# Rounded statistics of q and k and a new order of work in the opening of a hybrid decoder layer

## What is computed

```python
h = rmsnorm(x, g_mix)
q_sb, k_sb, v_sb, q_r, k_r, v_r, g_r, gate_sb, gate_ret = split_cols(h @ w_in)
q_sb = head_rmsnorm(to_heads(q_sb, SB_HEADS), sb_q_gain)      # 8 heads of 64
k_sb = head_rmsnorm(to_heads(k_sb, SB_HEADS), sb_k_gain)
y_sb = from_heads(stick_breaking_attention(q_sb, k_sb, to_heads(v_sb, SB_HEADS)))
q_r = rotary(to_heads(q_r, RET_HEADS)); k_r = rotary(to_heads(k_r, RET_HEADS)) * 0.125
y_r = retention_chunkwise(q_r, k_r, to_heads(v_r, RET_HEADS))
```

## Time and profile before

| | us |
|---|---|
| median of 3 runs (897.35 to 898.05) | 897.39 |
| the profiled execution's own time | 897.31 |
| its span, first to last instruction | 895.5 |
| TensorE busy | 887.5 (99%) |
| VectorE busy | 512.4 (57%) |
| ScalarE busy | 398.2 (44%) |
| GpSimd busy | 16.6 (2%) |

### The profile page before, as it was taken

One profiled execution on the slowest core, in us unless ns is written; L12 is line 12 of the kernel. 1 busy time (PEld: TensorE's weight loads), 2 busy tenths in 40 slices (PEclk: granted clock), 3 DMA queues, 4 the chain that ended last, 5 costly groups with the idle time before them and its releaser, 6 DMA issues.

```text
span 895.5 us, 11762 instructions
## 1 busy us (share of the span) xinstructions
PE 887.5 (99%) x4254; PEld 734.0 (82%) x4254; DVE 512.4 (57%) x644; ACT 398.2 (44%) x510; POOL 16.6 (2%) x19
## 2 busy tenths in 40 slices
PE   8999999999999999999999999999999999999998
PEld 6688888888888888888888888888888888888886
DVE  6797677677677443333556656566655643333444
ACT  6745756756755623232345333333333332323431
POOL 1500000000000000000000000000000000000000
PEclk9999999999999999999999999999999999999999
DMA  7224115115114252333223333322223333323141
GB/s 278 83 67 146 51 39 170 53 38 167 53 38 145 97 185 83 94 93 117 95 95 117 96 100 104 99 94 94 94 94 98 96 94 89 106 88 94 65 147 65
DMA packets 28699, 89.96 MB, mean 100 GB/s; under 512 B 3936, under 2 KB 5232, under 8 KB 28544
## 3 DMA queue, kind: packets, MB, share of 16 engines
q1 hardware_dynamic: 27376, 85.87, 30.1%
q10 hardware_dynamic: 1072, 3.67, 1.3%
q0 software_dynamic: 224, 0.06, 0.1%
HBM read 84.34 MB, written 2.10 MB: 97 GB/s over the span
## 4 chain that ended last, share of the span: by engine, by line
PE 96%; DVE 1%; DMA 1%; ACT 1%; issue 0%; SPq 0%; DVEq 0%
PE dense L424 30%; PE dense L426 29%; PE dense L425 29%; PE z L485 2%; PE aty L514 1%; DMA fs<-in_xT 1%; PE aty L425 1%; PE aty L426 1%; PE aty L424 1%; PE aty L529 1%; PE aty L531 1%; DVE fs L1228 0%; DVE w_lo L1228 0%; DVE lo L1231 0%; ACT hi L759 0%
## 5 line engine op out<-in xcount | busy, mean ns | idle before, releaser
L424 PE MATMUL dense<-hi,w_hi 128*128 128x512 f32 x1118 | 441.2, 395 | 1.4 <-DVE lo L1231 1.2
L425 PE MATMUL dense<-lo,w_hi 128*128 128x512 f32 x1118 | 435.4, 389 | 0.0
L426 PE MATMUL dense<-hi,w_lo 128*128 128x512 f32 x1118 | 435.3, 389 | 0.0
L1228 DVE TENSOR_TENSOR w_lo<-w_f,w_hi 128x1024 fp32r<-128x1024 f32 (+3 forms) x161 | 184.6, 1149 | 228.8 <-ACT w_hi L774 228.2
L424 PEld LDWEIGHTS dense<-hi,w_hi 128*128 128x128 f32 x1118 | 209.9, 188 | 50.7 <-issue 5.8
L426 PEld LDWEIGHTS dense<-hi,w_lo 128*128 128x128 f32 x1118 | 209.9, 188 | 44.4
L425 PEld LDWEIGHTS dense<-lo,w_hi 128*128 128x128 f32 x1118 | 210.1, 188 | 41.8 <-issue 0.7
L774 ACT CAST w_hi<-w_f 128x1024 fp32r<-128x1024 f32 (+2 forms) x159 | 157.5, 991 | 176.4 <-PE dense L426 174.3
L1228 DVE TENSOR_TENSOR fs<-fs 128x512 f32<-128x512 f32 (+3 forms) x115 | 86.8, 760 | 4.3 <-DMA fs<-fs 1.2
L759 ACT ACTIVATE fs<-fs 128x512 f32<-128x512 f32 (+2 forms) x75 | 54.5, 731 | 50.5 <-DVE fs L1231 38.6
L1228 DVE TENSOR_TENSOR lo<-fs,hi 128x512 fp32r<-128x512 f32 (+3 forms) x67 | 50.5, 762 | 37.2 <-ACT hi L1161 20.2
(11 more groups left out here) (118 smaller groups left out, 506.5 us busy)
## 6 DMA issues: line engine op xcount, KB each, us to landing
w_f<-in_w_in SPq DMA_DIRECT2D x52, 512.0 KB, 3.4
w_f<-in_w_up SPq DMA_DIRECT2D x44, 512.0 KB, 3.3
w_f<-in_w_down SPq DMA_DIRECT2D x16, 512.0 KB, 3.5
w_f<-in_w_b SPq DMA_DIRECT2D x8, 512.0 KB, 3.3
w_f<-in_w_out SPq DMA_DIRECT2D x8, 512.0 KB, 3.4
w_f<-in_w_pg SPq DMA_DIRECT2D x8, 512.0 KB, 3.3
w_f<-in_w_down SPq DMA_DIRECT2D x8, 384.0 KB, 3.1
fs<-in_xT SPq DMA_DIRECT2D x4, 512.0 KB, 7.3
```

Source lines behind the costliest of these rows:

```text
L424: mm(out, w1, x1, start=start, stop=False, skip_group_check=skip)
L425: mm(out, w1, x0, start=False, stop=False, skip_group_check=skip)
L426: return mm(out, w0, x1, start=False, stop=stop, skip_group_check=skip)
L1228: return nc.vector.tensor_tensor(out, a, b, op).then_inc(done, 1)
```

## The change

- The sums over the heads' squares of raw q and k are made in two rounded passes: ScalarE squares each twice, once rounded into `hi[:, T_FSQ + t]` and once in full, VectorE subtracts to `lo[:, T_FSQ + t]` (`first_square_low`), and TensorE multiplies both by the rounded block matrix `block_r`. That matrix is cast early, behind `raw_sum(3)`.
- TensorE makes the first of these sums behind block 1 of chunk 2 (before: behind block 6 of chunk 1), the second behind block 2 of chunk 2 (before: block 1). Five hooks of the first pair's `back` are one block later.
- On ScalarE `raw_square(0)` goes behind the rounding of chunk 1's weights, and `ahead(0, 2)` (chunk 4's weights) behind the split of q and k and the table load.
- On VectorE `constants()` and `ahead(0, 2)` go behind the norms, the split of q and k and the evacuation of v; only the scaled gain stays ahead.

```diff
--- before.py
+++ after.py
@@ -57,6 +57,7 @@
 T_AT = 27
 T_YQ = 27
 T_SQ = 31
+T_FSQ = 30
 T_X0 = 8
 T_M = 20
 T_G = 8
@@ -154,7 +155,7 @@
         s_rst, s_rln, s_rrs = sem("s_rst"), sem("s_rln"), sem("s_rrs")
         s_achi, s_aclo = sem("s_achi"), sem("s_aclo")
         s_w1hi, s_w1lo = sem("s_w1hi"), sem("s_w1lo")
-        s_fsq, s_xvar, s_fvar = sem("s_fsq"), sem("s_xvar"), sem("s_fvar")
+        s_fsq, s_fsqlo, s_xvar, s_fvar = sem("s_fsq"), sem("s_fsqlo"), sem("s_xvar"), sem("s_fvar")
 
         s_halo, s_c0, s_c1, s_c2, s_gelu = sem("s_halo"), sem("s_c0"), sem("s_c1"), sem("s_c2"), sem("s_gelu")
         s_g, s_ghi, s_glo = sem("s_g"), sem("s_ghi"), sem("s_glo")
@@ -453,9 +454,9 @@
 
             def first_stat(t):
 
-                pe.wait_ge(s_cst, 16)
-                pe.wait_ge(s_fsq, t + 1)
-                mm(z[:, t, :], cst[:, C_BLOCK, :], first_square(t), start=True, stop=True).then_inc(s_stat, 1)
+                pe.wait_ge(s_fsqlo, t + 1)
+                mm(z[:, t, :], block_r[:, :], hi[:, T_FSQ + t, :], start=True, stop=False)
+                mm(z[:, t, :], block_r[:, :], lo[:, T_FSQ + t, :], start=False, stop=True).then_inc(s_stat, 1)
 
             def stat_y(j):
 
@@ -614,10 +615,10 @@
                     return lambda: f(*a)
 
                 if prev is None:
-                    places = {(3, 0): at(sb_scores, j, 0), (3, 2): at(turn_v, 0, 2, (s_misc, 2)),
-                              (3, 7): at(sb_scores, j, 1), (4, 0): at(sb_turn, j, 0), (4, 5): at(sb_values, j, 0, 3),
+                    places = {(3, 1): at(sb_scores, j, 0), (3, 3): at(turn_v, 0, 2, (s_misc, 2)),
+                              (3, 7): at(sb_scores, j, 1), (4, 0): at(sb_turn, j, 0), (4, 6): at(sb_values, j, 0, 3),
                               (5, 1): at(sb_scores, j, 2), (5, 2): at(sb_turn, j, 1), (6, 0): at(sb_values, j, 0, 2),
-                              (6, 2): at(sb_turn, j, 2), (6, 5): at(sb_values, j, 0, 1), (6, 6): at(sb_values, j, 0, 0)}
+                              (6, 2): at(sb_turn, j, 2), (6, 6): at(sb_values, j, 0, 1), (6, 7): at(sb_values, j, 0, 0)}
                     first = 7
                 else:
                     places = {(3, 3): at(turn_v, j, 2, (s_misc, 3 * j + 1)), (3, 4): at(sb_scores, j, 0),
@@ -648,8 +649,8 @@
 
             warm_up()
             chunk(0, 0, 0, KD, T_X0, before={k: (s_xlo, k + 1) for k in range(KD)})
-            chunk(1, 1, 1, KD, T_X0, {6: lambda: first_stat(0)}, before={4: (s_wlo, 2)}, halved=True)
-            chunk(2, 2, 2, KD, T_X0, {0: stat_x, 1: lambda: first_stat(1)})
+            chunk(1, 1, 1, KD, T_X0, before={4: (s_wlo, 2)}, halved=True)
+            chunk(2, 2, 2, KD, T_X0, {0: stat_x, 1: lambda: first_stat(0), 2: lambda: first_stat(1)})
             back(0, None)
             with pe.Fori(1, PAIRS) as j:
                 front(j, j - 1, SLOTS * j)
@@ -782,6 +783,7 @@
 
             def first_square_of(t):
                 act.wait_ge(s_used, t + 1)
+                run(hi[:, T_FSQ + t, :], bank[t][:, :], ACT.Square, s_fsq)
                 run(first_square(t), bank[t][:, :], ACT.Square, s_fsq)
 
             act.wait_ge(s_gmix, 16)
@@ -791,11 +793,10 @@
                 if k % 2 == 0:
                     act.wait_ge(s_x[k // 2], 16)
                 run(hi[:, T_X0 + k, :], fs[:, A_X + k, :], ACT.Identity, s_xhi, scale=gain[:, G_MIX + k, :])
-                if k == 5:
-                    raw_square(0)
             act.wait_ge(s_wdma[1], 16)
             nc.scalar.copy(w_hi[1][:, 0:4, :], w_f[1][:, 0:4, :]).then_inc(s_w1hi, 1)
             nc.scalar.copy(w_hi[1][:, 4:8, :], w_f[1][:, 4:8, :]).then_inc(s_whi, 1)
+            raw_square(0)
             raw_square(1)
             raw_square(2)
             high(0, 2, first=True)
@@ -947,9 +948,9 @@
 
                 ahead(0, 1)
                 first_square_of(1)
-                ahead(0, 2)
                 act.wait_ge(s_xst, 1)
                 run(fs[:, A_G + 1, :], misc, ACT.Identity, s_xvar, scale=EPS * 64 / D)
+                act.wait_ge(s_fsqlo, 1)
                 run(fs[:, A_RS, :], misc, ACT.Ln, s_xln, scale=1.0 / D, bias=eps[:, :])
                 first_log(0)
                 act.wait_ge(s_xln, 1)
@@ -960,6 +961,7 @@
                 high_qk(0, 0)
                 high_qk(0, 1)
                 sigmoid_tables()
+                ahead(0, 2)
 
             def high_h(k):
                 act.wait_ge(s_hf, H_ORDER.index(k) + 1)
@@ -1270,21 +1272,33 @@
             low(0, 2)
             raw_sum(2)
             raw_sum(3)
+            dve.wait_ge(s_cst, 16)
+            nc.vector.tensor_copy(block_r[:, :], cst[:, C_BLOCK, :]).then_inc(s_cr, 1)
+
+            def first_square_low(t):
+
+                dve.wait_ge(s_fsq, 2 * t + 2)
+                if t == 0:
+                    dve.wait_ge(s_cr, 1)
+                tt(lo[:, T_FSQ + t, :], first_square(t), hi[:, T_FSQ + t, :], ALU.subtract, s_fsqlo)
+
+            first_square_low(0)
             low(1, 0)
-            def constants():
-
-                dve.wait_ge(s_cst, 16)
-                nc.vector.tensor_copy(ones_r[:, :], cst[:, C_ONES, :]).then_inc(s_cr, 1)
-                nc.vector.memset(mrev[:, 0:SEQ], 0.0).then_inc(s_cr, 1)
-                dve.wait_ge(s_cr, 2)
-                tt(mrev[:, 1:P + 1], cst[:, C_IDENT, ::-1], cst[:, C_IDENT, ::-1], ALU.mult, s_cr)
-                stt(cst[:, C_NEGU, :], cst[:, C_NEGU, :], 1.0, cst[:, C_IDENT, :], ALU.add, ALU.add, s_cr)
-                nc.vector.tensor_copy(block_r[:, :], cst[:, C_BLOCK, :]).then_inc(s_cr, 1)
-                dve.wait_ge(s_xacc, 3)
-                nc.vector.memset(fs[:, A_CP:A_CP + 2, 0:1], 0.0).then_inc(s_cr, 1)
+            first_square_low(1)
+            def scaled_gain():
+
                 dve.wait_ge(s_gain, 16 * 5)
                 g8 = gain[:, G_SBQ:G_SBQ + PAIRS, 0]
                 nc.vector.tensor_scalar(g8, g8, 0.125, None, ALU.mult).then_inc(s_cr, 1)
+
+            def constants():
+
+                nc.vector.tensor_copy(ones_r[:, :], cst[:, C_ONES, :]).then_inc(s_cr, 1)
+                nc.vector.memset(mrev[:, 0:SEQ], 0.0).then_inc(s_cr, 1)
+                dve.wait_ge(s_cr, 4)
+                tt(mrev[:, 1:P + 1], cst[:, C_IDENT, ::-1], cst[:, C_IDENT, ::-1], ALU.mult, s_cr)
+                stt(cst[:, C_NEGU, :], cst[:, C_NEGU, :], 1.0, cst[:, C_IDENT, :], ALU.add, ALU.add, s_cr)
+                nc.vector.memset(fs[:, A_CP:A_CP + 2, 0:1], 0.0).then_inc(s_cr, 1)
 
             def low_h(k):
                 dve.wait_ge(s_hhi, H_ORDER.index(k) + 1)
@@ -1469,15 +1483,17 @@
             def start():
                 first_variance(0)
                 first_variance(1)
-                constants()
-                dve.wait_ge(s_cr, 7)
-                ahead(0, 2)
+                scaled_gain()
+                dve.wait_ge(s_cr, 2)
                 first_norm(0)
                 first_norm(1)
                 low_qk(0, 0)
                 low_qk(0, 1)
                 dve.wait_ge(s_xrs, 1)
                 evac_x(2)
+                constants()
+                dve.wait_ge(s_cr, 7)
+                ahead(0, 2)
                 dve.wait_ge(s_rope, 16)
 
             def turned(j, t):
```

## The result

| | before | changed |
|---|---|---|
| median of 17 runs, us | 897.78 (897.29 to 898.35) | 900.19 (898.67 to 900.94) |
| ratio, 95% interval | | 1.0025 (1.0018 to 1.0033) |
| span of the profiled execution | 895.5 | 897.4 |
| mean granted clock of TensorE | 1.000 | 0.997 |

The changed kernel is 2.4 us slower, outside the range that was given (896.0 to 899.7). The mean clock of its executions is the first clue: two of the 17 have 1.000 and take 898.67 and 898.73 us, the other fifteen have 0.996 to 0.998 and take 899.20 to 900.94.

What follows compares the result with a forecast made beforehand. TensorE, busy 887.5 of 895.5 us, was the bound, with VectorE without slack from 34.40 to 59.8. VectorE's 1.0 us late minus 0.44 slack plus 0.2 restart gave +0.8: 897.31 to 898.1 us, range 896.0 to 899.7.

Steps and rivals of the forecast that it cites:

- the term for TensorE's clock: A lower TensorE clock behind the idle time at the second scores; left out of the forecast sum, priced at 1.8 us.
- rival 3: The 2.9 us stall at the second scores throws TensorE's clock to its lower level: 1.8 us more, 899.9 us, chance 0.08.
- The x part: Opening: moving ScalarE's first square of x behind the second chunk's rounding brings TensorE's start at 13.88 forward by 0.7 us.
- The new wait: TensorE reaches the sum of x squared at 20.8, VectorE's sum ends at 21.16: 0.4 us of new stall.
- Turns: Behind the norms, four moved VectorE instructions each wait for GpSimd's current instruction, up to 1.26 us; scans start 1.45 us late.
- Rivals 1 and 2: Cast waits for nothing: 896.9 us, chance 0.2. Short instructions not held up by GpSimd, or only by remainders: 895.9, chance 0.1.
- The idle stretch: TensorE waits at the second scores for the scans, from 35.3 to about 38.2, about 2.9 us.
- The sum without the clock: Everything behind the retention values' product comes 0.8 us later, giving 898.1 us, with nothing for a lower clock; chance 0.5.
- The low half of h: VectorE, behind the scans: 0.8 to 1.1 us late by this instruction, taken as 1.0.
- the term of 0.2 for a restart: TensorE's weight pipeline restarts behind a stall: 0.2 us added to the sum.
- A sign that failed: VectorE's evacuation ahead of the retention values was to come near 60.8 for 59.8.
- Rival 4: Memory set also waits for a GpSimd turn, and the product behind the scans loses its turn: +2.3, 899.6 us, chance 0.08.

Runs made afterwards that it cites:

- e11: The changed kernel again as it is, on the same chip as e12: 899.97 us, ratio 1.0024 to the kernel before.
- e12: The changed kernel with twelve unused products on TensorE ahead of the second scores, run again on the chip of e11: 898.01 us, ratio 1.0001.
- e1: The changed kernel with twelve unused products on TensorE ahead of the second scores, first run: 898.08 us, ratio 1.0003.
- e8: The kernel before with two memory sets of unused rows on VectorE ahead of the scans, so that TensorE idles: 903.34 us, ratio 1.0057.
- e4: The kernel before with only the first square of x moved behind the second chunk's rounding: 896.80 us, ratio 0.9991.
- e7: The changed kernel with GpSimd's products held back until the first two scans are done, one execution: 899.42 us.
- e6: The changed kernel with only the cast of the ones moved ahead of the first norm on VectorE: 897.41 us, ratio 0.9997.
- e10: The kernel of e3 again, on the chip of e9: 896.09 us, ratio 0.9978 to the kernel before.
- e3: The changed kernel with the constants on VectorE back ahead of the first norm, chunk 4's weights left behind the evacuation: 895.99 us, ratio 0.9979.
- e5: The changed kernel with five unused products on TensorE ahead of the second scores, leaving 1.8 us idle: 899.47 us, ratio 1.0017.
- e9: The kernel before with the moved square of x, chunk 4's weights behind the norms and later hooks, without rounded sums: 895.66 us, ratio 0.9975.

## Why the prediction was wrong

- **The failed step is the term for TensorE's clock, which the sum put at nothing.** The text had the mechanism as rival 3 and priced it (1.8 us, in all 899.9), but gave it 0.08 and set the range's end below it. It happened in 15 of 17 executions, and it costs 1.6 to 2.0 us (e11 against e12, and the executions of the changed kernel with and without it). That idle time is the cause is shown from both sides: filled with products the loss goes (e1, e12), and idle time alone brings the lower clock to the kernel before (e8). The reason given against it was that no slow products followed the wait at the first scores. That was one row of 1.1 us (the text's 1.2 is the sum of two other waits in the earlier trace rows) used for a stretch of 2.9: no row of the trace stood between them, and the slow warm-up products showed that this kernel can run at the lower level. The Trainium skill, TensorE: Matmul & The Clock Gate, section Why this matters for your kernels, advises against idle gaps between bursts of matmuls. The trace of the changed kernel agrees (2.9 us idle, then 0.50).
- **The x part** came as said: 0.7 forecast, 1.1 measured alone by the medians and 0.8 between the profiles (e4). The text named the wrong row for it. The 0.7 in the earlier trace rows is the wait at the first row of x; the product at 13.88 idles 0.51, and it starts 0.68 later than one block behind 12.97 would. The two sizes agree by luck.
- **The new wait** at the sum of x squared: 0.4 forecast, 0.6 in the profile. First norm: 26.75 and 26.88. First scores: 29.6 and 29.73.
- **Turns.** Forecast walk and profile: cast done 31.0 and 31.2, first operation 32.35 and 32.51, second 33.65 and 33.81, chunk 35.9 and 36.05, scans 35.85 and 35.97. The bound that was chosen, that each waits for the rest of a GpSimd instruction, is shown by e7 (gone without GpSimd) and e6 (one cast less, 1.24 us less). Rivals 1 and 2 fall.
- **The idle stretch**: forecast 2.9 us from 35.3 to 38.2, profile 2.89 from 35.46 to 38.35.
- **The sum without the clock** was 0.8 us. The filled kernels give 0.06 and 0.16 by the medians (e12, e1), with intervals that take 0.8 in, and the three executions without a fall of the clock 0.3 to 0.95. Where the difference lies is not shown, for executions of one kernel differ by 0.4 us before the norms: the first norm starts at 27.08 in e1's profile and at 26.65 in e12's, the same kernel, since rows of x land later in e1's. The low half of h, taken as 1.0 us late, is 1.06 late in e1's, 0.63 in e12's and 0.85 in that of the changed kernel, all against the one profile of before. The scans are 1.35 late in e12's, and the multiplication behind them, which waited 0.7 us for GpSimd in the kernel before (1.92 us), no longer does (1.22). The retention values' product starts at 60.88 (e1) and 60.44 (e12) for 60.25, and these executions take 0.77 and 0.30 us more than the profiled 897.31. That execution, the start of the walk, lies 0.5 to 0.6 under the medians of the larger samples (897.78 to 897.95). The forecast of 898.1 so meets the filled kernels' 898.08 and 898.01 in part by luck of its base. No row was given for the term of 0.2 for a restart; in the earlier trace rows's profile the product behind the stall at 13.88 comes 0.34 and not 0.23 behind it (at 14.22), which gives 0.1.
- **A sign that failed.** The evacuation ahead of the retention values was to come near 60.8. It ends at 61.90 in the changed kernel, and at 60.83 in e1, where the clock stays up.
- **Rival 4** falls with the memory set's unchanged 0.48 us and with the product behind the scans, which has its free 1.22.

## What to carry to other kernels

A gain ahead of a stretch in which another engine has no gap turns into idle time at the stretch's entry, and idle time of TensorE is not free: here 1.6 to 3.3 us of it were followed, in some or most executions, by 3.4 to 6.8 us at half the clock. Before work is moved behind something, look at what runs beside it there; three small instructions of 0.8 us in sum made about 2 us of difference by whether GpSimd was running (e12 against e10, e1 against e3), and 3.9 with the clock (e11 against e10). And where a forecast makes an idle stretch longer than any in the trace, treat the clock as open, or fill the stretch, as twelve useless products did here.

## What the runs showed that was not expected

- The clock's fall is not the same in each execution of one kernel: 2.9 us of idle time lowered it in 25 of 28 executions of the changed kernel, 1.8 us in 6 of 11 (e5), 1.6 us in 4 of 11 (e6), 3.3 us in 3 of 4 (e8), and 2.9 us filled with products in none of 22 (e1, e12). This counts by the mean clock of each execution.
- The stretch at the lower level lasted 3.4 us in three profiles (the changed kernel and e11 behind 2.9 us of idle time, e6 behind 1.6) and 6.8 us in that of e8, behind 3.3. It began 0.7 to 1.3 us after TensorE had taken up its work again in the three, and 0.7 before it in e8.
- The warm-up's 18 products, the same in every kernel, took 5.7 us in e6's profile and 7.2 in e9's.
- A cast of 128 columns takes turns with GpSimd (1.01 us for 0.22). The Trainium skill, SBUF — State Buffer, section Who interferes with whom, says it may; no row of the trace before had shown it.
- The 0.8 us that rounded sums save TensorE brought nothing that the time shows (e9 against e10), though TensorE is 99% busy.
